# The forget gate's summed rows: eight transfers within SBUF in place of matmuls and copies

## The chip, the cores and the metric

One core of one Trainium2 chip. The metric is the device time of one execution in microseconds (us), the median of the runs shown.

## The reference, cut to what matters

A stack of layers in float32 for 512 tokens: an even layer (forget-gate attention and latent attention), an odd layer, two convolutional feed-forward parts, a delta-rule layer and an MLP. The change lies in the even layer's attention with a forget gate. Eight heads of width 64; each head has one gate value for each token, and the running sum of its logarithm enters every score:

```python
log_f = jax.nn.log_sigmoid((fg + b_forget).astype(jnp.float32))
...
c = jnp.cumsum(log_f, axis=1).transpose(0, 2, 1)
...
logits = jnp.einsum('bqhd,bkhd->bhqk', qb, k).astype(jnp.float32) * scale
logits = logits + cq[..., :, None] - c[..., None, :]
logits = jnp.where(mask, logits, NEG_INF)
p = jax.nn.softmax(logits, axis=-1).astype(v.dtype)
```

The term cq is the same for a whole row of the softmax and drops out; the kernel adds only the negated sum by key, `-c[k]`. A tile of scores has queries on the partitions and keys along the free dimension, so each of its 128 partitions needs the same row of 512 values, a different one for each head.

## The kernel before, in words

Activations lie with features on the partitions, x and hH/hL as [128, 8, 512]. Products in float32 are made of three matmuls on rounded high and low parts (`three`, lines 474 to 476). Weights come in units of up to 1024 KB: SP loads a unit into one of two raw buffers (line 406) as soon as the split of the unit that used it is done (semaphore w_split), ACT rounds it to wH (two halves, `even_hi`), DVE subtracts to wL (`lo_half`, line 2022), PE multiplies.

The order of the even layer is written out by hand as slots. PE walks t from 32 to 239; each t is one step of a projection (for even_in one of eight k steps of a tile, 16 slots a unit), and pair_events(t) puts the attention's work ahead of that step. ACT and DVE walk the same t from 34 on with their parts of the same slots. A tile of attention is a pair of heads g = m // 4 and a block of 128 queries, largest first: m = 0 to 15 are the forget-gate heads, pair_slot(m) = 48, 55, 62, 69 for the first pair, 76, 83, 90, 97 for the second, 104, 111, 118, 125 for the third, 147 and on for the fourth. At slot s PE makes both heads' scores (`pair_scores`, L749, mask L754), after waiting that DVE is done with head 1 of the tile before (line 729, event pair.biased); DVE adds the bias and takes the row's minimum (`pair_biased`, L2306), waiting for gate.bias of both heads; ACT takes the exponential at s + 1; DVE divides at s + 4 (L2315, L2317, events pair.prob); at s + 7 PE transposes (`pair_turn`, L767), ACT copies, and after four tiles PE multiplies by the values (L778).

The bias. DVE's gate chain (lines 2347 to 2359) runs on eight partitions, one for each head: minimum, log-sigmoid with ACT's help, a running sum along the tokens (L2356), a negation (L2357). The negated sums are rounded by ACT and the remainder made by DVE (L2359), into gate_split, two float32r rows for each head. At gate_slot(h) = 43, 45, 66, 68, 88, 90, 106, 108, PE spreads head h to all partitions (`gate_spread`, L788 and L789): the row is picked by a column of the identity, in two matmuls over 8 partitions, into bank 7; ACT copies the bank to cB (`gate_bias`), which has room for two pairs of heads. From the third pair on ACT first waits until pair.biased of the last tile of the pair two before is there, since its row of cB is written again. `a`, ACT's helper, is line 1330 for all of its activations. `rank_sums`, at slot 116, uses bank 7 next and waits for the last gate.bias.

Other transfers that stay inside SBUF: at slot 146 ACT issues two (line 1650) that copy the rotated key rows, 32 partitions, into kM, four times each; SP issues eight of 32 partitions into qM (line 450). ACT's queue also carries rope (line 1579), dist and the constants of the later layers.

Of the kernel before, what the change touches and what calls it, by code (L numbers as in the profile page):

```python
# [21 lines left out]
F32 = mybir.dt.float32  # L22
F32R = mybir.dt.float32r
# [4 lines left out]
P = 128  # L28
# [69 lines left out]
class Events:  # L98
# [22 lines left out]
    def at(self, event, i=None):  # L121
        if self.known is None:
            return self.sem("first_build"), 1
        name, value, stride = self.known[event]
        if i is None:
            return self.sem(name), value
        return self.sem(name), i * stride + value
# [26 lines left out]
def build(nc, dram, known):  # L154
    ctx = ExitStack()
    with ctx:
# [7 lines left out]
        def sb(name, shape, dt=F32, where=None):  # L164
            size = 4 * int(np.prod(shape[1:]))
            if where is None:
                where = place[0]
                place[0] += size
            assert where + size <= nc.sbuf_usable_end, (name, where + size - nc.sbuf_usable_end)
            return nc.alloc_sbuf_tensor_at(name, shape, dt, offset=where)  # L170
# [34 lines left out]
        cq_at, qF_at = base + 4 * 5 * SEQ, base + 4 * (13 * SEQ + 2 * 1280)  # L205
        cqRaw = sb("cqRaw", [P, 5, SEQ], F32, cq_at)
        foxH, foxL = sb("foxH", [P, 4, SEQ], F32R, qF_at), sb("foxL", [P, 4, SEQ], F32R, qF_at + 4 * 4 * SEQ)
        gate_split = sb("gate_split", [P, 2, SEQ], F32R, qF_at + 4 * 16 * SEQ)
        qM, kM = sb("qM", [P, H, SEQ], F32, h_at), sb("kM", [P, H, SEQ], F32, h_at + 4 * H * SEQ)
        mH, mL, ft = stage([("mH", [P, MLP_GROUP, SEQ], F32R), ("mL", [P, MLP_GROUP, SEQ], F32R), ("ft", [P, 8, SEQ])])  # L210
        vO, dist, probO, lamt, dH, dL, qk = stage([
# [70 lines left out]
        def gate_slot(h):  # L282
            return (43, 66, 88, 106)[h // 2] + 2 * (h % 2)
# [184 lines left out]
        def _(pe):  # L468
# [310 lines left out]
                                  start=j == 0, stop=j == TT - 1, skip_group_check=True)  # L779
                last.then_inc(*tick("pair_pe", f"pair.values{g}"))  # L780

            def gate_spread(h):

                pe.wait_ge(*at("gate.rows"))
                if h:
                    pe.wait_ge(*at(f"gate.bias{h - 1}"))
                pick = identR[0:H, h:h + 1].to_broadcast([H, P])
                mm(bank[7][:], pick, gate_split[0:H, 0, :], start=True, stop=False)  # L788
                mm(bank[7][:], pick, gate_split[0:H, 1, :], start=False, stop=True).then_inc(*tick("gate_pe", f"gate.spread{h}"))  # L789

            def rank_sums():

                pe.wait_ge(*at(f"gate.bias{H - 1}"))
                for c, what in enumerate(("cq", "ckv")):
                    pe.wait_ge(*at(f"{what}.squares"))
                    for t in range(TT):
                        last = mm(bank[7][:, 4 * c + t:4 * c + t + 1], (sq[:, 0, :], ss)[c][:, t * P:(t + 1) * P], ones[:, 0:1],
                                  start=True, stop=True)
                last.then_inc(*tick("sums_pe", "cq.sums"))

            def pair_events(t):

                for m in pairs_at(t, 0):
                    pair_scores(m)
                for g in pair_ends(t, 9):
                    pair_values(g)
                for m in pairs_at(t, 7):
                    pair_turn(m)
                for h in range(H):
                    if gate_slot(h) == t:  # L810
                        gate_spread(h)

            def first_ready(k):

# [513 lines left out]
        def _(act):  # L1328
# [249 lines left out]

            act.dma_start(rope[:], dram["rope"]).then_inc(*tick("loaded_rope", "in.rope", 16))

            act.wait_ge(*at("gate.min"))
            gate_log = prob[0:H, 0, 0:512]
            a(gate_log, misc[0:H, :], ACT.Abs, bias=v("b_forget")[0:H, :]).then_inc(*tick("gate_act", "gate.abs"))
# [1 line left out]
            a(gate_log, gate_log, ACT.Exp, scale=-1.0).then_inc(*tick("gate_act", "gate.exp"))  # L1585
            act.wait_ge(*at("gate.exp"))
            a(gate_log, gate_log, ACT.Ln, bias=1.0).then_inc(*tick("gate_act", "gate.ln"))
            act.wait_ge(*at("gate.negative"))
            a(gate_split[0:H, 0, :], prob[0:H, 1, 512:1024], ACT.Copy).then_inc(*tick("gate_act", "gate.hi"))

            def even_hi(n, f):

# [21 lines left out]
            def pair_hi(g):  # L1614

                act.wait_ge(*at(f"pair.values{g}"))
                a(foxH[:, g, :] if g < 4 else hH[:, 2 * g - 8, :], bank[6][:], ACT.Copy).then_inc(*tick("pair_act", f"pair.hi{g}"))

            def gate_bias(h):

                act.wait_ge(*at(f"gate.spread{h}"))
                if h >= 4:
                    act.wait_ge(*at(f"pair.biased{4 * (h // 2 - 2) + 3}.1"))
                a(cB[:, h // 2 % 2, h % 2, :], bank[7][:], ACT.Copy).then_inc(*tick("gate_act", f"gate.bias{h}"))

            def rank_square(k):

# [6 lines left out]
            for t in range(34, 240):  # L1634
# [32 lines left out]
                        pair_copy(m)  # L1667
                for m in pairs_at(t, 1):
                    pair_exp(m)
                for h in range(H):  # L1670
                    if gate_slot(h) == t:
                        gate_bias(h)
                for m in pairs_at(t, 7):
# [328 lines left out]
        def _(dve):  # L2002
# [342 lines left out]
                tt(sq[:, g, :], sq[:, g, :], ss[:], ALU.add).then_inc(*tick("rope_dve", f"rope.rotated{g}"))  # L2345

            even_evict(0)
            gate_log, gate_z, gate_one, gate_neg = (prob[0:H, e, 512 * c:512 * c + 512] for e in range(2) for c in range(2))
            dve.wait_ge(evac, 1)
            nc.vector.memset(gate_one, 1.0)  # L2350
            chain(ts(gate_z, misc[0:H, :], v("b_forget")[0:H, :], 0.0, ALU.add, ALU.min), "gate_dve", "gate.min")
# [2 lines left out]
            dve.wait_ge(*at("gate.ln"))  # L2354
            chain(tt(gate_z, gate_z, gate_log, ALU.subtract), "gate_dve", "gate.logf")
            chain(nc.vector.tensor_tensor_scan(gate_log, gate_one, gate_z, 0.0, ALU.mult, ALU.add), "gate_dve", "gate.summed")  # L2356
            ts(gate_neg, gate_log, -1.0, None, ALU.mult).then_inc(*tick("gate_dve", "gate.negative"))  # L2357
            dve.wait_ge(*at("gate.hi"))
            tt(gate_split[0:H, 1, :], gate_neg, gate_split[0:H, 0, :].bitcast(F32), ALU.subtract).then_inc(*tick("gate_dve", "gate.rows"))  # L2359
            for t in range(34, 240):  # L2360
                if t % 8 == 0 and 40 <= t <= 144:
                    even_evict(t // 8 - 1)
# [651 lines left out]
```

## Time and profile before

| | us |
|---|---|
| median of 3 runs | 2013.41 |
| lowest, highest | 2012.32, 2014.16 |
| span of the profiled execution | 2010.4 |
| PE busy | 1991.0 |
| DVE busy | 1149.2 |
| ACT busy | 820.8 |
| POOL busy | 3.8 |

The profiled execution is given by its span, from its first to its last instruction; the median of the runs is 3.0 us more, which is what lies around a span. The mean granted clock of PE is 0.998. PE's matmul durations overlap: two matmuls of 0.39 us start 0.23 us apart, so positions are read by starts. Line 1330 stands for every ACT activation; tiles tell them apart.

### The profile page before, as it was taken

Reading aid. Unit: us, or ns where it says so; the run is one execution under the profiler, and the core shown is the slowest. Engines: PE = TensorE matmul, PEld = TensorE weight load, DVE = VectorE, ACT = ScalarE, POOL = GpSimd, SP = SyncE. Lnnn points to the kernel's source line nnn. Section 1 sums busy time; section 2 is a strip of 40 time slices with the busy share of each in tenths; the row PEclk is TensorE's granted clock in tenths of the full one; section 3 lists DMA queues with packets and bytes.
Section 4 is the critical chain, followed back from the end, with each engine's and each line's share of the span. In section 5 each row is a group of like instructions: output and inputs, shape, how many; then the busy total and the mean of one; then the engine's idle time right before and its main releaser. Section 6 shows DMA issues by size and latency. Waiting matters only on the chain.

```text
span 2010.4 us, 30047 instructions
## 1 busy us (share of the span) xinstructions
PE 1991.0 (99%) x11917; PEld 1608.7 (80%) x11917; DVE 1149.2 (57%) x1896; ACT 820.8 (41%) x1293; POOL 3.8 (0%) x6
## 2 busy tenths in 40 slices
PE   9999999999999999999999999999999999999998
PEld 6776798888888787888888888777777578888888
DVE  6456467534556666567543555877666566424532
ACT  6447544333334454454332333643443432212322
POOL 0000000000000000000000000000000000000000
PEclk9999999999999999999999999999999999999999
DMA  5112122223323211122223224111111122322221
GB/s 192 64 53 84 43 85 92 86 95 105 104 79 110 69 64 64 63 85 86 97 95 102 102 77 142 42 62 33 57 43 44 45 84 103 105 87 102 88 100 63
DMA packets 26992, 165.58 MB, mean 82 GB/s; under 512 B 3200, under 2 KB 3328, under 8 KB 11008
## 3 DMA queue, kind: packets, MB, share of 16 engines
q1 hardware_dynamic: 25872, 161.69, 23.4%
q10 hardware_dynamic: 1008, 2.30, 0.4%
q8 instruction: 82, 1.34, 0.3%
q14 instruction: 30, 0.25, 0.0%
HBM read 160.83 MB, written 2.10 MB: 81 GB/s over the span
## 4 chain that ended last, share of the span: by engine, by line
PE 89%; DVE 6%; ACT 3%; issue 1%; DMA 0%; SPq 0%; DVEq 0%; ACTq 0%
PE bank L474 25%; PE bank L476 24%; PE bank L475 24%; PE bank L1133 2%; PE bank L749 1%; ACT hH L1330 1%; DVE hL L2102 1%; PE bank L957 1%; PE bank L778 1%; PE bank L981 1%; ACT wH L1330 1%; DVE x L2098 1%; PE bank L767 1%; PE bank L1222 1%; PE bank L1220 1%
## 5 line engine op out<-in xcount | busy, mean ns | idle before, releaser
L474 PE MATMUL bank<-hH,wH 128*128 128x512 f32 x1368 | 552.0, 404 | 1.5 <-DVE hL L2064 1.5
L476 PE MATMUL bank<-hH,wL 128*128 128x512 f32 x1368 | 533.7, 390 | 0.0
L475 PE MATMUL bank<-hL,wH 128*128 128x512 f32 x1368 | 533.1, 390 | 0.0
L1330 ACT ACTIVATE wH<-raw 128x2048 fp32r<-128x2048 f32 (+3 forms) x199 | 294.1, 1488 | 116.3 <-PE bank L476 105.1
L474 PEld LDWEIGHTS bank<-hH,wH 128*128 128x128 f32 x1368 | 257.6, 188 | 69.0 <-issue 14.5
L476 PEld LDWEIGHTS bank<-hH,wL 128*128 128x128 f32 x1368 | 257.4, 188 | 54.4
L475 PEld LDWEIGHTS bank<-hL,wH 128*128 128x128 f32 x1368 | 257.9, 189 | 46.1
L2013 DVE TENSOR_TENSOR wL<-raw,wH 128x2048 fp32r<-128x2048 f32 x96 | 219.7, 2289 | 125.6 <-ACT wH L1330 125.6
L474 PE MATMUL bank<-mH,wH 128*128 128x512 f32 (+1 forms) x610 | 233.1, 382 | 0.0
L476 PE MATMUL bank<-mH,wL 128*128 128x512 f32 (+1 forms) x610 | 232.9, 382 | 0.0
L475 PE MATMUL bank<-mL,wH 128*128 128x512 f32 (+1 forms) x610 | 232.9, 382 | 0.0
L474 PEld LDWEIGHTS bank<-mH,wH 128*128 128x128 f32 x610 | 114.7, 188 | 22.2
L475 PEld LDWEIGHTS bank<-mL,wH 128*128 128x128 f32 x610 | 114.7, 188 | 22.0
L476 PEld LDWEIGHTS bank<-mH,wL 128*128 128x128 f32 x610 | 114.7, 188 | 22.0
L1330 ACT ACTIVATE y<-bank 128x512 f32<-128x512 f32 (+4 forms) x132 | 57.8, 464 | 150.3 <-PE bank L476 89.0
L2022 DVE TENSOR_TENSOR wL<-raw,wH 128x1024 fp32r<-128x1024 f32 x76 | 92.0, 1218 | 22.3 <-ACT wH L1330 22.1
L2418 DVE TENSOR_TENSOR ft<-bank,dg 128x512 f32<-128x512 f32 x44 | 30.4, 690 | 86.2 <-PE bank L476 86.2
L1330 ACT ACTIVATE ft<-ft 128x512 f32<-128x512 f32 x44 | 27.8, 632 | 116.6 <-DVE ft L2423 116.6
L1330 ACT ACTIVATE ft<-ft,vec 128x512 f32<-128x512 f32 x44 | 35.8, 815 | 86.5 <-DVE ft L2418 86.5
L1330 ACT ACTIVATE mH<-y 128x512 f32 (+1 forms) x32 | 20.2, 632 | 120.9 <-DVE y L2841 120.9
L1330 ACT ACT_TABLE_LOAD x47 | 60.3, 1283 | 1.7 <-PEq L3005 0.7
L474 PE MATMUL bank<-wH,hH 128*128 128x256 f32 x192 | 57.5, 299 | 0.0
(346 smaller groups left out, 2790.5 us busy)
## 6 DMA issues: line engine op xcount, KB each, us to landing
raw<-in_ffn_up SPq DMA_DIRECT2D x44, 1024.0 KB, 4.8
raw<-in_mlp_up SPq DMA_DIRECT2D x16, 1024.0 KB, 4.9
raw<-in_mlp_down SPq DMA_DIRECT2D x16, 1024.0 KB, 4.9
raw<-in_ffn_down SPq DMA_DIRECT2D x16, 768.0 KB, 4.2
raw<-in_odd_in SPq DMA_DIRECT2D x12, 1024.0 KB, 4.8
raw<-in_dn_qkv SPq DMA_DIRECT2D x12, 1024.0 KB, 4.9
raw<-in_ffn_down SPq DMA_DIRECT2D x16, 640.0 KB, 3.8
raw<-in_even_in SPq DMA_DIRECT2D x7, 1024.0 KB, 4.8
```

The source lines that it names most:

```text
L474: mm(out, a, c, start=first, stop=False, skip_group_check=joined)
L475: mm(out, a, d, start=False, stop=False, skip_group_check=joined)
L476: return mm(out, b, c, start=False, stop=last, skip_group_check=joined)
L749: last = mm(bank[2 + e][:, 0:n], q, k, start=True, stop=g >= 4)
L767: last = nc.tensor.transpose(bank[4 + e][:, j * P:(j + 1) * P], pair_tile(e, i)[:, j * P:(j + 1) * P], ident)
L778: last = mm(bank[6][half(e), j * P:], (vF if g < 4 else vM)[:, j, head(g % 4, e)], PT[:, e, j, j * P:], start=j == 0, stop=j == TT - 1, sk ...
L957: last = mm(bank[2 + e][:, 0:n], qk[half(e), h % 2, 0, i * P:n], qk[half(e), h % 2, 1, 0:n], start=True, stop=True)
L1133: last = mm(bank[b][part(e), chunk(n)], left[part(e), chunk(n)], right[part(e), chunk(n)], start=True, stop=True)
L1330: return nc.scalar.activation(out, in_, func, **kw)
L2013: tt(wL[s][:], raw[s][:], wH[s][:].bitcast(F32), ALU.subtract).then_inc(w_split, 1)
L2022: ins = tt(wL[n % 2][:, cols], raw[n % 2][:, cols], wH[n % 2][:, cols].bitcast(F32), ALU.subtract)
L2418: tt(gate, bank[b0][:], rinv, ALU.mult).then_inc(evac, 1)
```

## The change

gate_split becomes gate_rows, a plain float32 tile, into whose first eight partitions DVE writes the negated sums. ACT's rounding and DVE's subtraction go. PE's gate_spread goes, and with it the wait of rank_sums. gate_bias(h) on ACT is no longer a copy from PSUM: it issues a transfer from partition h of gate_rows, repeated 128 times, to the same place in cB (256 KB). The first four are issued in one go right behind the gate chain, ahead of ACT's first slot; heads 4 to 7 keep their slots 88, 90, 106 and 108 and their wait. Each transfer has its own semaphore, which counts 16. DVE's waits in pair_biased are the same events.

```diff
-        gate_split = sb("gate_split", [P, 2, SEQ], F32R, qF_at + 4 * 16 * SEQ)
+        gate_rows = sb("gate_rows", [P, SEQ], F32, qF_at + 4 * 16 * SEQ)
...
-            def gate_spread(h):
-
-                pe.wait_ge(*at("gate.rows"))
-                if h:
-                    pe.wait_ge(*at(f"gate.bias{h - 1}"))
-                pick = identR[0:H, h:h + 1].to_broadcast([H, P])
-                mm(bank[7][:], pick, gate_split[0:H, 0, :], start=True, stop=False)
-                mm(bank[7][:], pick, gate_split[0:H, 1, :], start=False, stop=True).then_inc(*tick("gate_pe", f"gate.spread{h}"))
-
             def rank_sums():
 
-                pe.wait_ge(*at(f"gate.bias{H - 1}"))
...
-                for h in range(H):
-                    if gate_slot(h) == t:
-                        gate_spread(h)
...
+            def gate_bias(h):
+
+                if h >= 4:
+                    act.wait_ge(*at(f"pair.biased{4 * (h // 2 - 2) + 3}.1"))
+                act.dma_start(cB[:, h // 2 % 2, h % 2, :], gate_rows[h:h + 1, :].unsqueeze(1).to_broadcast([1, P, SEQ]))\
+                    .then_inc(*tick(f"gate_loaded{h}", f"gate.bias{h}", 16))
+
...
-            act.wait_ge(*at("gate.negative"))
-            a(gate_split[0:H, 0, :], prob[0:H, 1, 512:1024], ACT.Copy).then_inc(*tick("gate_act", "gate.hi"))
+            act.wait_ge(*at("gate.rows"))
+            for h in range(4):
+                gate_bias(h)
...
-            def gate_bias(h):
-
-                act.wait_ge(*at(f"gate.spread{h}"))
-                if h >= 4:
-                    act.wait_ge(*at(f"pair.biased{4 * (h // 2 - 2) + 3}.1"))
-                a(cB[:, h // 2 % 2, h % 2, :], bank[7][:], ACT.Copy).then_inc(*tick("gate_act", f"gate.bias{h}"))
...
-                for h in range(H):
+                for h in range(4, H):
                     if gate_slot(h) == t:
                         gate_bias(h)
...
-            ts(gate_neg, gate_log, -1.0, None, ALU.mult).then_inc(*tick("gate_dve", "gate.negative"))
-            dve.wait_ge(*at("gate.hi"))
-            tt(gate_split[0:H, 1, :], gate_neg, gate_split[0:H, 0, :].bitcast(F32), ALU.subtract).then_inc(*tick("gate_dve", "gate.rows"))
+            ts(gate_rows[0:H, :], gate_log, -1.0, None, ALU.mult).then_inc(*tick("gate_dve", "gate.rows"))
```

## Rows read from the trace of the kernel before

**Rows 1.** The page: span, busy time of the engines.

```profile
span 2010.4 us, 30047 instructions
PE 1991.0 (99%) x11917; PEld 1608.7 (80%) x11917; DVE 1149.2 (57%) x1896; ACT 820.8 (41%) x1293; POOL 3.8 (0%) x6
```

**Rows 2.** Window in the even layer: length, busy time and count of PE, PEld, DVE, ACT, POOL, then PEclk, DMA share, GB/s.

```profile
46.00:56.00 10.00, 10.00 (x79) 8.72 (x76) 6.58 (x15) 5.59 (x12) 0.00 (x0) 1.00 0.12 48
```

**Rows 3.** Instructions of line 788: durations in ns, first and last start in us.

```profile
L788 PE MATMUL bank<-gate_split,constR x8: 475/493/497, 40.4 to 111.3; 8*128 8x512 f32 x8
```

**Rows 4.** Timeline of PE around the second spread: start, us, engine, line, what.

```profile
42.07 0.39 PE L475 MATMUL bank<-hL,wH 128*128 128x512 f32 x1
42.30 0.40 PE L476 MATMUL bank<-hH,wL 128*128 128x512 f32 x1
...
43.62 0.39 PE L475 MATMUL bank<-hL,wH 128*128 128x512 f32 x1
```

**Rows 5.** Timeline of ACT: the gate's rounding and the wH of unit 3.

```profile
38.98 0.63 ACT L1330 ACTIVATE gate_split<-prob 8x512 fp32r<-8x512 f32 x1 [2.44 <-DVE prob L2357]
39.52 1.99 ACT L1330 ACTIVATE wH<-raw 128x1024 fp32r<-128x1024 f32 x2
```

**Rows 6.** Timeline of ACT: the two issues of line 1650, and what stood behind them.

```profile
150.20 1.38 ACTq L1650 DMA_DIRECT2D kM<-misc  x2
151.63 0.59 ACT L1330 ACTIVATE kM<-bank 64x512 f32<-64x512 f32 x1 [1.72 <-issue]
```

**Rows 7.** Timeline of DVE, from the split of unit 3 to head 3 of the second group.

```profile
40.59 2.36 DVE L2022 TENSOR_TENSOR wL<-raw,wH 128x1024 fp32r<-128x1024 f32 x2 [0.27 <-ACT wH L1330]
...
47.59 0.69 DVE L2306 CUSTOM_DVE_ANT_0 prob<-bank,cB 128x512 f32<-128x512 f32 x1
...
49.47 0.89 DVE L2317 TENSOR_SCALAR prob<-prob,stat 128x512 f32<-128x512 f32 x2
...
58.43 0.75 DVE L2317 TENSOR_SCALAR prob<-prob,stat 128x384 f32<-128x384 f32 x2
...
75.68 0.69 DVE L2306 CUSTOM_DVE_ANT_0 prob<-bank,cB 128x512 f32<-128x512 f32 x1
```

**Rows 8.** Timeline of PE: first step of unit 3, transposes of tiles 0 and 1.

```profile
46.88 0.33 PE L474 MATMUL bank<-wH,hH 128*128 128x256 f32 x1
...
53.18 1.06 PE L767 MATMUL bank<-const,prob 128*128 128x128 f32 x8
...
60.10 0.84 PE L767 MATMUL bank<-const,prob 128*128 128x128 f32 x6
```

**Rows 9.** DMA issues of the whole run: tile, queue, count, KB each, median us from issue to landing.

```profile
qM<-sq SPq DMA_DIRECT2D x8, 64.0 KB, 2.0
kM<-misc ACTq DMA_DIRECT2D x2, 256.0 KB, 3.7
dist<-in_dist ACTq DMA_DIRECT2D x1, 256.0 KB, 2.5
raw<-in_even_in SPq DMA_DIRECT2D x7, 1024.0 KB, 4.8
```

**Rows 10.** Windows: both kM transfers in flight, a 1024 KB weight load.

```profile
152.00:152.50 0.50, 0.50 (x4) 0.46 (x5) 0.20 (x1) 0.49 (x2) 0.50 (x2) 1.00 0.94 180
177.00:178.00 1.00, 1.00 (x6) 0.73 (x4) 0.42 (x2) 0.99 (x4) 0.00 (x0) 1.00 0.98 418
```

**Rows 11.** Window at the end of the run, behind the last matmul.

```profile
2008.00:2009.00 1.00, 0.00 (x0) 0.00 (x0) 0.00 (x0) 0.00 (x0) 0.00 (x0) 0.50 1.01 410
```

**Rows 12.** Timelines of ACT, DVE and PE at the third group.

```profile
88.89 0.60 ACT L1330 ACTIVATE cB<-bank 128x512 f32<-128x512 f32 x1 [2.28 <-PE bank L789]
...
106.42 0.68 DVE L2306 CUSTOM_DVE_ANT_0 prob<-bank,cB 128x512 f32<-128x512 f32 x1
...
108.28 0.88 DVE L2317 TENSOR_SCALAR prob<-prob,stat 128x512 f32<-128x512 f32 x2
...
115.37 1.06 PE L767 MATMUL bank<-const,prob 128*128 128x128 f32 x8
```

More of the change, by code:

```diff
@@ L2347, in _ @@
             even_evict(0)
-            gate_log, gate_z, gate_one, gate_neg = (prob[0:H, e, 512 * c:512 * c + 512] for e in range(2) for c in range(2))
+            gate_log, gate_z, gate_one = (prob[0:H, c // 2, 512 * (c % 2):512 * (c % 2) + 512] for c in range(3))
             dve.wait_ge(evac, 1)
```

## The prediction

> **What bounds the kernel now.** The page comes first: PE is busy 1991.0 of 2010.4 us, no other engine over 57% [rows 1]. A window inside the even layer says the same of the stage that is changed: PE busy all of 10 us, at clock 1.00, with 48 GB/s on the DMA engines [rows 2]. So PE's instruction stream is the clock of this stage, and what PE doesn't execute is time gained, as long as nothing that PE waits for comes later. Then come the timelines of each engine from 38 to 62 us, and the table of DMA issues. The profiled execution is known by its span, 2010.4 us; the median of the three runs is 3.0 us above it, and I carry that 3.0 along.
>
> **What is removed.** The first spread runs at 40.4, the last at 111.3 us, eight in all [rows 3]. In PE's timeline two matmuls of the projection start 0.23 us apart; around a spread, from L476 at 42.30 to the L475 two places on, 1.32 us pass where 0.46 would [rows 4]. So a spread costs 0.86 us, with the switches to and from eight-row weights. Two spreads lie ahead of the first group's softmax: 1.7 us. Six lie behind it; three of them stand beside transposes, scores or values, where PE pays a switch anyway (I take off 0.1 each): 4.8 us. In all 6.5 us of PE time. ACT loses one rounding (0.63 us [rows 5]) and eight copies of 0.60 us, DVE one subtraction; both have idle time, so I count nothing for these. rank_sums loses a wait that was long satisfied: nothing.
>
> **What is added on ACT's queue.** The first four transfers are issued in a row as soon as the negated sums are there, where the rounding began, at 38.98 us [rows 5]. Two issues took 1.38 us and the next activation waited behind them [rows 6]. Four take 2.8, so ACT is at 41.8 where it was at 39.52 [rows 5]. Queued behind them on ACT: both halves of wH of unit 3 (2.0 us), on which DVE's split waits (2.36 us from 40.59 [rows 7]); it would end about 45.2 instead of 42.95. PE wants unit 3 at 45.2 (46.88 [rows 8] less two spreads), so the price is 0 to 0.2 us and disappears in what comes next. SP's next weight load is released by the same split and comes 2.3 us later; it takes 4.8 us [rows 9] and its data are used 20 us on: nothing. The table puts no transfer of SP beside the first two, and POOL has nothing here.
>
> **How long a transfer takes.** This is the price that decides. All of the 256 KB of one transfer are read from one partition (row h, 128 times 2 KB). The trace has no such transfer, so it is bounded. Fixed part: 64 KB within SBUF land 2.0 us after the issue [rows 9]; I take 2.0. Moving part, lower bound: the rate of a load into 128 partitions, 418 GB/s [rows 10], 0.6 us; dist, with the same 256 KB in the same rows of 2 KB, lands in 2.5 [rows 9]. The nearest rows are the two kM transfers: inside SBUF, the same queue, 2 KB pieces, each source row read four times, but 32 partitions on either side. There the DMA engines are busy 0.94 of the time and yet move 180 GB/s, less than half of 418 [rows 10], and they land in 3.7 [rows 9]. So with fewer partitions the sixteen engines stand in each other's way. Upper bound: in proportion to partitions, 180/32 = 5.6 GB/s, 47 us. Between: 128 to 32 partitions cost a factor 2.3; the same factor for each further fourfold step (two and a half of them) gives 180/8.0 = 22 GB/s, and a sixteenth of 418, one engine's share, is 26. I take **26 GB/s, 10 us for a transfer**, since both ways of going on from the nearest rows come out near it (11.7 by the other).
>
> The Trainium skill, page "SBUF — State Buffer", section "Door 1: The DMA port swizzle", says that a transfer's rate depends on how many of 16 ports its partitions reach, 8 for 32 partitions and one for four or fewer, and gives 27.6 GB/s measured for partitions 0 to 3. By it a transfer would move for an estimated 9.5 us and the sum would be 1 us less. The halving in the kM rows agrees with it; that reading alone, with writes spread over all partitions, obeys it too is shown by no row.
>
> **Where it lands on the path.** The transfers share one queue and neighbouring source partitions, so they follow each other and land at 39.0 + 2.0 + 10, 20, 30, 40, that is at 51, 61, 71 and 81 us. DVE needs the second for head 1 of the first tile (L2306 at 47.59 [rows 7]). It waits until 61. Behind it on DVE stand the division of tile 0, the split of unit 4, an eviction and the second tile; ACT waits for DVE with the exponential, and behind that the wH of unit 4. PE waits first in the scores of tile 1 (line 729) at about 50.5, then in the transposes of tile 0. In the trace the products end 2.77 us after the start of that L2306 (47.59 to 50.36 [rows 7]), so 63.8 now; the transposes of head 0 may start 0.4 earlier, at 63.4, against 53.18 before [rows 8]: **+10.2 us**. DVE then still has the splits of unit 4, an eviction and the rotary of the keys between it and the products of tile 1; those ended at 59.18 [rows 7], 0.9 before PE used them at 60.10 [rows 8], and I estimate them 1.3 us later against PE: +0.4.
> PE stands still for some 11 us. At the end of the run, in a window without a matmul, its clock is granted at 0.50 (1.2 of 2.4 GHz) [rows 11], where it was 1.00 in the layer [rows 2], so it will come back from the stall at the lower level. No row shows how soon it rises again. Bounds: 0, and all of the 6.9 us from tile 0's transposes to tile 1's [rows 8] at half speed, 6.9. I take 2, nearer the low end, because part of that stretch is semaphore and switch time, which a clock doesn't stretch.
> Second group (heads 2, 3, landed at 81): first wanted both at 75.68 [rows 7], now later by 10.6 + 2 - 1.7: 87. Hidden. Third group: ACT can issue head 4 at about 86.6, where it now begins to wait (88.89 - 2.28 [rows 12]), head 5 behind the square of the second tile; both have landed 22 us later, at 108.6 on the old scale. The spreads of heads 4 and 5 are gone from in between, so on that scale DVE wants them at 104.7, not 106.42, and waits 3.9. The products end 2.74 us after the bias (109.16 less 106.42 [rows 12]), now at 111.3, and PE, four spreads earlier than 115.37 [rows 12], wants them at 112.0: 0.7 in hand. SP loads weights in the same stretch, so I count +0.5. Fourth group: over 35 us of lead, nothing.
>
> Sum: + 10.2 + 0.4 + 2 + 0.5 - 4.8 (the six later spreads; the first two are inside the 10.2) = **+8.3 us**: span 2018.7, time 2021.7.
>
> **The rivals.**
> - **Hidden (faster).** Only writing suffers from few partitions, and the kM rows, which have 32 on both sides, can't tell. Then a transfer moves in 0.6 to 1.4 us, the first two land by 44, DVE needs them at 46 at the soonest, and the 6.5 us of spreads come out less 0.2: 2007.1. It decides in this way as long as head 1 lands before 49 (PE's transposes of tile 0 at 53.18 less 1.7, less the 2.4 from landing to transposes), that is below 4 us a transfer; the change breaks even at some 6.5. For it: kM's 3.7 us to landing, and that nothing else loads in that stretch. Against it: engines 0.94 busy at less than half the rate. The Trainium skill, page "DMA: Bandwidth & Descriptors", section "Anatomy of one DMA", gives (for the gpsimd path) 2.0 us plus bytes over 436 GB/s, an estimated 2.6 us for 256 KB; dist in the trace agrees, kM does not.
> - **One partition is much slower than a sixteenth.** At 20 us a transfer head 1 lands at 81 (+30.6), heads 2 and 3 at 121 where 107 is wanted (+14), the third group waits 24 less 4.6 of slack (+19), the fourth +1; with clock and spreads +62: 2075. Against it: it needs a limit that the kM rows do not show.
> - **Not what it says.** If the broadcast were read once and written 128 times, it is the hidden case.
>
> **How the numbers follow.** A sixteenth of the rate or near it: 0.58; hidden: 0.28; much slower: 0.10; break-even, some 6.5 us a transfer: 0.04. About 0.2% (4 us) is what a measurement can tell. Faster 0.30 (the hidden case and half of the break-even), within 0.2% 0.04 (the rest, and the low edge of the likeliest), slower 0.66. The likeliest case reaches from 2017 (9 us a transfer, no clock) to 2036 (about 13 us: +6 at head 1, +5 at the third group, 2 more for the clock). The range has to take in the hidden case as well: 2006 to 2036, with the much slower case left out.
>
> **What would show it.** Landing times of the first four transfers in steps of 10 us, with the DMA share near 1 at about 26 GB/s; L2306 waiting for the transfers from 46 to 61; PE idle about 11 us before line 749 of tile 1, the granted clock below 1 behind it; no stall at the second group. PE's stream 6.5 us shorter and no gap would make the prediction wrong, and so would landing times of 3 us. If PE waited for wL of unit 3, the four issues would be the price.

## The result, and the profile after

| | before | after |
|---|---|---|
| median | 2013.66 (4 runs) | 2025.04 (4 runs) |
| lowest, highest | 2012.32, 2014.16 | 2023.58, 2026.65 |
| span of the profiled execution | 2010.4 | 2024.8 |

The changed kernel is slower: ratio 1.0057, with a 95% interval of 1.0044 to 1.0070, or +11.4 us by the medians. The two profiled executions differ by 14.4 us in span. The one of after is the longest of its four runs (2026.65 us) and 1.85 us above its span; in the other runs of both kernels, too, the time is only some 1.8 to 2.2 us above the span. So not all of the 3.0 us that the prediction carried lies around a span: about one is that the execution of before was a short one, and some 3 us of the 14.4 are scatter. The forecast was +8.3.

The page of after, where [rows 1] stood before:

```profile
span 2024.8 us, 30001 instructions
...
PE 1987.4 (98%) x11901; PEld 1609.3 (79%) x11901; DVE 1148.4 (57%) x1895; ACT 816.0 (40%) x1284; POOL 3.8 (0%) x6
...
PE bank L474 25%; PE bank L476 23%; PE bank L475 23%; PE bank L1120 2%; PE bank L749 1%; ACT hH L1317 1%; DVE hL L2090 1%; PE bank L944 1%; ACT wH L1317 1%; PE bank L778 1%; PE bank L968 1%; ACTq L1572 1%; DVE x L2086 1%; PE bank L767 1%; PE bank L1209 1%
```

PE is busy 3.6 us less and the span is 14.4 us longer. In the chain by line, a DMA issue of ACT has come in, ACTq L1572, which is the transfer of gate_bias. So time is lost in issuing. The transfers by tile (line, queue, count, durations of the issues in ns, first and last start in us; below, from issue to landing):

```profile
L1572 ACTq DMA_DIRECT2D cB<-gate_rows x8: 477/600/9608, 38.7 to 123.1; - x8
...
DMA to landing us min/median/max: 11.8/18.6/32.6
```

One issue took 9.6 us where 0.7 was reckoned (half of the 1.38 of [rows 6]). The chain that ended last, in order of time, from the gate chain to the first scores (start, us, what):

```profile
38.65 0.59 ACTq L1572
39.28 0.61 ACTq L1572
39.92 6.77 ACTq L1572
46.71 9.61 ACTq L1572
56.42 1.06 ACT wH L1317
57.51 0.98 DVE wL L2010
58.50 0.16 issue
58.65 1.23 DVE wL L2010
59.93 2.08 PE bank L749 x4
```

Two issues pass in 0.6 us each, the third holds ACT for 6.8, the fourth for 9.6: 17.7 us in all. Behind them on ACT stands the wH of unit 3, behind it on DVE the split to wL, and behind that PE. Its timeline (start, us, engine, line, tiles; in brackets the idle time before and what ended it):

```profile
43.05 0.39 PE L476 MATMUL bank<-hH,wL 128*128 128x512 f32 x1
59.93 2.08 PE L749 MATMUL bank<-kF,qF 64*128 64x512 f32 x4 [16.49 <-DVE wL L2010]
...
70.38 1.06 PE L767 MATMUL bank<-const,prob 128*128 128x128 f32 x8
```

PE stands still for 16.5 us. The transposes of tile 0 come at 70.38, at 53.18 before [rows 8]. Windows of the stretch (columns as in rows 2):

```profile
46.00:50.00 4.00, 0.00 (x0) 0.00 (x0) 0.00 (x0) 0.00 (x0) 0.00 (x0) 0.50 0.88 27
50.00:52.00 2.00, 0.00 (x0) 0.00 (x0) 0.00 (x0) 0.00 (x0) 0.00 (x0) 0.50 0.95 29
...
64.00:66.00 2.00, 2.00 (x12) 2.00 (x11) 1.24 (x4) 2.00 (x4) 0.00 (x0) 0.50 0.92 28
66.00:68.00 2.00, 2.00 (x18) 2.00 (x18) 0.95 (x1) 0.59 (x1) 0.00 (x0) 0.96 0.88 27
```

From 46 to 56 us all five engines are idle, and the DMA engines are some 0.9 busy for 25 to 29 GB/s. That is about the rate that was forecast. The granted clock is 0.50 in the stall and stays there for the first six microseconds of work.

The path can be followed by the starts of the transposes (L767), after less before. They stood at 53.18 and 115.37 before [rows 8, 12]; now at 70.38 and 127.56, so +17.2 and +12.2. The scores ahead of the first came 14.4 later (45.55 before, 59.93 now). So: 14.4 us by the stall, with two spreads already taken off; 2.8 more in the stretch at half clock; 5.0 given back by the six later spreads; and then, by the next transposes (124.07 before, 138.45 now), +14.4 again. These last 2.2 us are lost while heads 6 and 7, the fourth pair, are issued. ACT's timeline there, then PE's:

```profile
122.56 0.72 ACT L1317 ACTIVATE prob<-prob,stat 128x512 f32<-128x512 f32 x1 [1.50 <-DVE stat L2294]
122.56 6.93 ACTq L1572 DMA_DIRECT2D cB<-gate_rows  x2
...
129.60 1.09 ACT L1317 ACTIVATE y<-bank 128x512 f32<-128x512 f32 x2 [5.22 <-PE bank L767]
```

```profile
132.04 0.95 PE L787 MATMUL bank<-const,sq 128*128 128x1 f32 x8
133.51 1.05 PE L787 MATMUL bank<-const,ss 128*128 128x1 f32 x8 [0.52 <-DVE ss L2367]
```

The issue of head 7 takes 6.4 of the 6.93 us, the exponential of the next tile comes late, DVE's sum of squares behind it too, and PE waits 0.5 us; the granted clock is 0.61 and 0.54 in the four microseconds from 134 us. That this makes up the 2.2 us is read from this one trace: in the first experiment below head 7's issue is held 6.3 us in the same way, the clock stays at 1.00 from 126 to 136 us, and only 0.6 us are lost.

### The profile page after: what moved, and what is told of

The parts are those of the page before. It is cut to its first block, busy times and chain, and to the rows that moved or that the text cites. A ratio compares the mean times of both kernels' runs of the same rounds, so it can differ in the third digit from the quotient of the medians.

```text
span 2024.8 us, 30001 instructions
## 1 busy us (share of the span) xinstructions
PE 1987.4 (98%) x11901; PEld 1609.3 (79%) x11901; DVE 1148.4 (57%) x1895; ACT 816.0 (40%) x1284; POOL 3.8 (0%) x6
## 4 chain that ended last, share of the span: by engine, by line
PE 86%; DVE 6%; ACT 4%; issue 2%; ACTq 1%; DMA 1%; SPq 0%; DVEq 0%
PE bank L474 25%; PE bank L476 23%; PE bank L475 23%; PE bank L1120 2%; PE bank L749 1%; ACT hH L1317 1%; DVE hL L2090 1%; PE bank L944 1%; ACT wH L1317 1%; PE bank L778 1%; PE bank L968 1%; ACTq L1572 1%; DVE x L2086 1%; PE bank L767 1%; PE bank L1209 1%
```

## The experiments

Theory A, from the chain: a queue takes only so many slow transfers; the issues hold ACT, and that is the price. Theory B, the prediction's: the landing of head 1 holds DVE. A third question is what makes a transfer slow. Each edit is against the changed kernel unless another is named. Each ratio is to runs of the kernel before made beside that experiment, whose medians lie between 2013.03 and 2014.18 us.

Spans scatter for a reason far from the change. In a later layer, some 1305 us into the run, PE waits once for DVE's rowsG. Of the following lines the first is of the last experiment, the second of the first kernel with eight sources (who waits for whom, total, times, longest):

```profile
PE bank L1141 <- DVE rowsG L2619: 1.8, 1, 1.8
PE bank L1141 <- DVE rowsG L2618: 3.1, 1, 3.1
```

Where it is 3.1, the granted clock goes down to about 0.50 behind it, and from there to the end the run takes some 1.5 or 3.0 us more than the 701.6 of the others. It is 1.8 in the traces of before, after, the first and the last experiment and 3.1 in the nine others; what decides it wasn't looked into. So the table behind the last experiment compares the even layer alone.

### Two issued behind the gate chain, two later

```diff
-            for h in range(4):
+            for h in range(2):
                 gate_bias(h)
...
+                if t == 44:
+                    gate_bias(2)
+                    gate_bias(3)
```

> Only the place of the issues of heads 2 and 3 is changed: ACT issues heads 0 and 1 behind the gate chain, heads 2 and 3 at its slot 44, behind the rounding of unit 3. Theory A (a transfer from one partition moves at 26 to 29 GB/s, and ACT can't begin a third one before the first is nearly drained, so the four issues in a row held up the weights of unit 3): two issues of 0.6 us, unit 3 rounded by 42, no wait of PE for wL at slot 48; now the landing of head 1 at about 60 holds DVE, PE stands still before the scores of tile 1, its transposes of tile 0 start near 63.4 instead of 70.4 in the changed kernel, and the run is 4 to 7 us faster than the changed kernel, about 2018 to 2021. Theory B (the landing of head 1 at 60 binds anyway and the held issues cost nothing of their own): the same time as the changed kernel, within 1.5 us of 2025.

Measured: 2021.9 us, ratio 1.0041 [1.0027, 1.0056], span 2018.1. Timelines of DVE, PE and ACT:

```profile
51.13 0.69 DVE L2297 CUSTOM_DVE_ANT_0 prob<-bank,cB 128x512 f32<-128x512 f32 x1 [6.08 <-DMA cB<-gate_rows]
...
61.27 0.69 DVE L2297 CUSTOM_DVE_ANT_0 prob<-bank,cB 128x512 f32<-128x512 f32 x1 [9.44 <-DMA cB<-gate_rows]
```

```profile
62.02 1.65 PE L749 MATMUL bank<-kF,qF 64*128 64x384 f32 x4 [11.54 <-DVE stat L2297]
...
64.09 1.93 PE L767 MATMUL bank<-const,prob 128*128 128x128 f32 x8
```

```profile
40.52 6.58 ACTq L1572 DMA_DIRECT2D cB<-gate_rows  x1
...
47.13 8.92 ACTq L1572 DMA_DIRECT2D cB<-gate_rows  x1
```

The wait for wL is gone and the one that the prediction describes stands in its place: DVE waits until 61.3 (forecast 61), PE stands still 11.5 us in the scores of tile 1 (forecast some 11) and makes the transposes of tile 0 at 64.1 (forecast 63.4). The transposes of tile 1 are at 72.05 against 60.10 [rows 8], +12.0 where the prediction's terms give 12.6. The two later issues are held 6.6 and 8.9 us as before; they only no longer stand ahead of unit 3. Both mechanisms are real; the held issues hide the late landing, because the earlier stall lets head 1 arrive in time. Taking the first off the path saves 6.7 us of span, not 16. By the medians it is 2.5 us (+8.9 against +11.4, each to its own runs of before) where 4 to 7 were expected, and the two intervals overlap: that one stall takes the other's place is shown by the traces, its worth by them alone.

### A source on 128 partitions

```diff
-                act.dma_start(cB[:, h // 2 % 2, h % 2, :], gate_rows[h:h + 1, :].unsqueeze(1).to_broadcast([1, P, SEQ]))\
+                act.dma_start(cB[:, h // 2 % 2, h % 2, :], x[:, h, :])\
```

> The eight transfers keep their size, queue, order and destination, but read x (128 partitions, 2 KB of each) in place of one partition of the gate's rows, so the bias added to the scores is not the gate's. Theory A (the single source partition sets the rate, and the slow drain is what holds the issues): each lands in 2.5 to 3.7 us, each issue takes 0.5 to 0.7 us, PE has no wait in the even layer that it didn't have before, and the time is the before kernel's less the spreads, 2006 to 2008. Theory C (the rate is set by the writes, by the queue of ACT or by transfers inside SBUF as such): landings stay near 10 us apart and the time near 2025.

This kernel leaves out the gate's bias and adds x in its place; it is for timing alone, as are the next two. Measured: 2008.25 us, ratio 0.9974 [0.9963, 0.9985]. The transfers by tile, a window in which they are in flight, and PE's wait:

```profile
L1572 ACTq DMA_DIRECT2D cB<-x x8: 472/521/634, 38.6 to 104.9; - x8
...
DMA to landing us min/median/max: 2.3/2.5/5.1
```

```profile
40.00:41.00 1.00, 1.00 (x6) 0.80 (x6) 0.00 (x0) 0.00 (x0) 0.00 (x0) 1.00 1.01 379
```

```profile
PE bank L749 <- DVE wL L2010: 1.4, 1, 1.4
```

The same bytes to the same places at 379 GB/s, landed in 2.5 us, and no issue above 0.63. Now the change is a gain. The long issues come from the slow transfers, not from their number alone: four in a row took 2.5 us (forecast 2.8). But PE still waits 1.4 us for wL, where the prediction had 0 to 0.2.

### Four source partitions, side by side or four apart

```diff
+                act.dma_start(cB[:, h // 2 % 2, h % 2, :], x[0:4, h:h + 1, :].to_broadcast([4, P // 4, SEQ]))\
```

```diff
+                act.dma_start(cB[:, h // 2 % 2, h % 2, :], x[0:16:4, h:h + 1, :].to_broadcast([4, P // 4, SEQ]))\
```

> As e2, but the source is x on partitions 0 to 3, each row read 32 times; the bias is again not the gate's. Theory A1 (neighbouring partitions share one way out, as the page on the port swizzle has it): still 26 to 29 GB/s, landings 9 to 10 us apart, time near 2025. Theory A2 (each single partition has a limit of its own, about 28 GB/s): four times the rate, 256 KB in 2.3 us, landings near 4.5 us after the issue, time near 2007.

> As e3, but on partitions 0, 4, 8 and 12. Both A1 and A2 expect about 105 to 115 GB/s: 256 KB move in 2.3 to 2.5 us, landings 4.5 us after the issue, and a time near 2007 to 2009. If it is as slow as e3, the number of source partitions or of DMA engines used counts, and not which partitions they are.

Measured, one run each: 2021.22 us for partitions 0 to 3, 2011.28 for 0, 4, 8 and 12. A window with the transfers in flight, of the first and then of the second, and the four issues of the first:

```profile
42.00:44.00 2.00, 1.66 (x8) 1.04 (x6) 0.00 (x0) 0.00 (x0) 0.00 (x0) 1.00 0.23 25
```

```profile
40.00:41.00 1.00, 1.00 (x6) 0.84 (x5) 0.00 (x0) 0.00 (x0) 0.00 (x0) 1.00 0.26 102
```

```profile
38.86 9.92 ACTq L1572 DMA_DIRECT2D cB<-x  x4
```

Both keep about a quarter of the DMA engines busy (share 0.23 and 0.26), and the one moves 25, the other 102 GB/s. A single source partition, with a share of 0.8 to 1.0, moved 25 to 29 in most windows. So the limit is neither the engines nor the single partition, but a way out that four neighbouring partitions share: 25 to 29 GB/s, and four such ways 102. The Trainium skill, page "SBUF — State Buffer", section "Door 1: The DMA port swizzle", puts partitions 0 to 3 on one of 16 ports, with 27.6 GB/s, and 0, 4, 8 and 12 on four; these two windows agree with it, and for reads.

The issues don't follow the rate alone. The longest is 9.6 us for one partition, 4.1 for four side by side and 1.3 for four apart; but one partition and four side by side drain equally fast (25 to 29 and 25 GB/s), and yet the four issues take 17.7 us in the one case and 9.9 in the other. That is why the first of these kernels came out near 2021 and not at the 2025 that was expected: PE waits 8.7 us for wL in place of 16.5, and then the landing of head 1 is what binds, with tile 0's transposes at 64.08, as in the first experiment (64.09). The second is above its expectation of 2007 to 2009: four issues take 4.3 us and PE waits 3.1 for wL.

### Eight sources for each head

The gate's weight columns are laid out so that head h's gate comes out on eight partitions, four apart; the gate chain runs on 64 partitions in place of 8, at the same durations.

```diff
-                act.dma_start(cB[:, h // 2 % 2, h % 2, :], gate_rows[h:h + 1, :].unsqueeze(1).to_broadcast([1, P, SEQ]))\
+                o = 32 * (h // 4) + h % 4
+                act.dma_start(cB[:, h // 2 % 2, h % 2, :], gate_rows[o:o + 32:4, :].unsqueeze(1).to_broadcast([8, 16, SEQ]))\
...
-    misc = np.concatenate([w[:, cuts[2]:cuts[2] + 64], kr, kr[:, 16:], kr[:, :16]], 1)
+    copies = [4 * (p // 32) + p % 4 for p in range(64)]
+    misc = np.concatenate([w[:, cuts[2]:cuts[3]][:, copies], kr, kr[:, 16:], kr[:, :16]], 1)
```

> The changed kernel with one thing else: the weight columns of the gate are laid out so that each head's gate is computed on eight partitions four apart (64 partitions in all, the same instructions), and each transfer reads these eight, 16 times each. The result is the reference's. Theory A1 (partitions four apart have ways out of their own, 26 GB/s each): about 200 GB/s, 256 KB in 1.3 us, landings 3.3 to 3.7 us after the issue, four issues of 0.6 us in a row, PE waits 1.5 us for wL of unit 3 as in e2 and for nothing else new: 2007 to 2009, 0.2 to 0.3% faster than before. If something about a gate row that the chain has just written counts, and not its partitions: near 2020.

> e5 with heads 2 and 3 issued at ACT's slot 44, behind the rounding of unit 3, as in e1. By the account of e2 this takes 1.2 us off ACT's queue ahead of unit 3 and so most of PE's 1.5 us wait: 2006 to 2008, 1 us faster than e5. If the wait has another cause, the same as e5.

The second of the two also has heads 2 and 3 at slot 44, as in the first experiment. Measured: 2010.69 us, ratio 0.9982 [0.9973, 0.9992]; and 2007.57, 0.9968 [0.9956, 0.9981]. A window of the first, and its wait; then the wait of the second:

```profile
40.00:41.00 1.00, 1.00 (x6) 0.84 (x5) 0.00 (x0) 0.00 (x0) 0.00 (x0) 1.00 0.53 166
```

```profile
PE bank L749 <- DVE wL L2011: 2.3, 1, 2.3
```

```profile
PE bank L749 <- DVE wL L2014: 0.7, 1, 0.7
```

About half of the engines are busy and move 135 to 166 GB/s, less than twice the rate of four and below the 200 that was expected. The four issues take 3.4 us where four of 0.6 were expected. No wait for a landing is left; what remains is the wait for unit 3, which shrinks from 2.3 to 0.7 us when two issues move behind its first half. The longer wait costs more than its length. Behind it, in the first kernel:

```profile
46.00:48.00 2.00, 2.00 (x8) 1.25 (x7) 1.16 (x4) 0.00 (x1) 0.00 (x0) 0.50 0.93 271
```

In the second the clock is 1.00 in that window, and tile 0's transposes come at 51.47 where they are at 54.44 in the first, 3.0 us for 1.6 us less of waiting.

### By way of HBM

```diff
-                act.dma_start(cB[:, h // 2 % 2, h % 2, :], gate_rows[h:h + 1, :].unsqueeze(1).to_broadcast([1, P, SEQ]))\
+                act.dma_start(cB[:, h // 2 % 2, h % 2, :], gate_hbm[h:h + 1, :].unsqueeze(1).to_broadcast([1, P, SEQ]))\
...
+            act.dma_start(gate_hbm[:], gate_rows[0:H, :]).then_inc(*tick("gate_stored", "gate.stored", 16))
+            act.wait_ge(*at("gate.stored"))
```

> The changed kernel with the rows stored to HBM first (16 KB, one more transfer and a wait of ACT for it) and the eight transfers reading one row of HBM 128 times. If only a single SBUF partition is slow to read: the store lands at 41, each transfer moves at 200 to 400 GB/s and lands in 2.5 to 3.5 us, ACT is held for 2 us by the store and 2.4 by the issues, unit 3's wL is 3.5 to 4 us late at PE: about 2010. If repeated reads of one 2 KB place are slow wherever they are: landings 10 us apart, and above 2025.

Measured: 2010.81 us, ratio 0.9977 [0.9966, 0.9989]. Window:

```profile
43.00:44.00 1.00, 0.64 (x3) 0.19 (x1) 0.00 (x0) 1.00 (x2) 0.00 (x0) 1.00 1.00 354
```

One HBM row read 128 times moves at 354 GB/s, so a source read many times is not slow by itself; it is slow where it is one partition of SBUF. The store in front (issued at 38.85, first broadcast at 40.35) costs ACT 1.5 us, and PE waits 2.8 us for wL; the granted clock is 0.50 from 46 to 52 us behind it.

### Two heads by PE, six by slow transfers

The kernel before, with its spreads for heads 0 and 1 (both on gate_split as before), and heads 2 to 7 by the change's transfer from one partition, each at a slot of its own:

```diff
-                for h in range(H):
-                    if gate_slot(h) == t:
+                for h in range(H):
+                    if (43, 45, 46, 60, 78, 86, 100, 112)[h] == t:
                         gate_bias(h)
```

> The kernel before, in which only heads 2 to 7 come by the slow transfers from one partition, issued one at a time at ACT's slots 46, 60, 78, 86, 100 and 112, at least 8 us apart and 12 us or more before their use; heads 0 and 1 stay two spreads on PE. Theory A (the slow rate costs only where a landing or a held issue is on the path): six spreads less and nothing waits: 4 to 5 us faster than before, about 2008 to 2009, though each transfer still lands in 11 to 12 us. If slow transfers cost by themselves (by slowing the weight loads that share the engines): no gain, or slower.

Measured: 2008.36 us, ratio 0.9971 [0.9962, 0.9981]. The transfers by tile:

```profile
L1627 ACTq DMA_DIRECT2D cB<-gate_rows x6: 477/480/589, 43.1 to 111.3; - x6
...
DMA to landing us min/median/max: 11.1/11.3/12.2
```

One at a time, the same transfer is issued in 0.5 us and lands in 11.3, and nothing waits for it. Six spreads less give 5.1 us by the medians. A load of 1024 KB beside them landed after 12.7 us in place of 4.8, and that was hidden too. So it is not the slow transfer that costs, but its being wanted 8 us after the row is there, and its being issued where earlier ones have not drained.

### The four issues on SP's queue

```diff
+                        if n == 5:
+                            sp.wait_ge(*at("gate.rows"))
+                            for h in range(4):
+                                sp.dma_start(cB[:, h // 2 % 2, h % 2, :], gate_rows[h:h + 1, :].unsqueeze(1).to_broadcast([1, P, SEQ]))\
+                                    .then_inc(*tick(f"gate_loaded{h}", f"gate.bias{h}", 16))
...
-            for h in range(4):
-                gate_bias(h)
```

> The changed kernel with the first four transfers issued by SP, ahead of its load of unit 5, in place of ACT; source, size and order are the same. If it is the issuing queue that is held while earlier transfers of it drain: SP's third and fourth issue take 6.5 and 9 us in its turn, ACT rounds unit 3 at 39 at once, PE has no wait for wL at slot 48, and DVE waits for head 1 until 60 as in e1; transposes of tile 0 near 63.5; the load of unit 5 is issued 11 us late (56 in place of 45) and lands in time for ACT's slot 66. Time 2019 to 2022, about that of e1. If it is something of ACT: SP's issues take 0.6 us each.

Measured: 2027.15 us, ratio 1.0067 [1.0052, 1.0083]. The chain, SP's part of it, and PE's second stop:

```profile
40.35 6.75 SPq L443
47.14 9.59 SPq L443
56.77 26.38 DMA raw<-in_even_in
```

```profile
87.75 0.68 PE L772 MATMUL bank<-const,prob 128*128 128x128 f32 x2 [2.40 <-DVE prob L2308]
```

The holds are the same to 0.02 us on another engine's queue, so they come from the transfers and not from ACT. ACT is free now and the first stall is that of the first experiment (11.1 us). But SP's own next load, of unit 5, goes out at 56.8 in place of some 43, and lands 26.4 us later, behind the broadcasts of its own queue; a load takes 4.8 otherwise [rows 9]. ACT waits 8.65 us for it before it can round the unit, PE stops once more for 2.4 us, and its clock falls a second time (0.50 from 88 to 90 us). By the transposes of the next pair's first tile this kernel is 4.3 us behind the first experiment (98.08 and 93.83), from 0.6 ahead at tile 0. The expectation of 2019 to 2022 had no such second stop.

### PE kept at work through the stall

The first experiment, with 46 matmuls into an idle bank ahead of the scores of tile 1.

```diff
+                if t == 55:
+                    for n in range(46):
+                        mm(bank[7][:], hH[:, 0, 0:P], hH[:, 0, :], start=True, stop=True)
```

> e1 with 46 matmuls more on PE, written to bank 7 and used by nobody, ahead of the scores of tile 1, where PE stands still from 50.5 to 62 in e1. They take 46 x 0.227 = 10.4 us of a stall of 11.5. If the clock at 0.50 behind the stall costs time: the granted clock stays at 1.00 up to 61, the work from 62 to 66 runs at full speed, and the run is 2 us (1 to 3) faster than e1's 2021.9. If it costs nothing: within 0.7 us of e1, or slower by what the extra matmuls overrun.

Measured: 2021.08 us, ratio 1.0039 [1.0024, 1.0055], beside 1.0041 without them. Windows:

```profile
62.00:64.00 2.00, 1.61 (x8) 0.92 (x9) 1.08 (x6) 1.91 (x4) 0.00 (x0) 0.96 0.81 25
64.00:66.00 2.00, 2.00 (x12) 2.00 (x11) 2.00 (x5) 1.74 (x3) 0.00 (x0) 0.50 1.02 31
66.00:68.00 2.00, 2.00 (x14) 2.00 (x14) 1.97 (x5) 1.38 (x5) 0.00 (x0) 0.69 0.88 27
```

The clock stays up through the stall and falls all the same at 64, after two short stops at 61 and 63 us. From the scores of tile 1 to the transposes of tile 1 it is 10.1 us with the matmuls and 10.0 without (62.11 to 72.21, 62.02 to 72.05), and 8.05 in the kernel before (52.05 to 60.10). The dip moved; the run was 0.8 us faster where 1 to 3 was expected if the clock costs time and up to 0.7 if it doesn't, and it decides nothing, since the clock fell in both.

### Eight sources, all issued behind unit 3's first half

```diff
+                if t in (36, 44):
+                    for h in range(2):
+                        gate_bias(h + (t == 44) * 2)
```

With the sources of the eight-fold layout, and the issues ahead of ACT's first slot taken out.

> e6 with heads 0 and 1 issued behind ACT's rounding of unit 3 as well (ACT's slot 36; heads 2 and 3 at slot 44). PE's wait for wL of unit 3 (0.7 us in e6) goes; heads 0 and 1 are issued at about 41 and land at 44.5 to 45.5, ahead of DVE's use at 46. By this account 2006 to 2008, up to 1 us faster than e6. If the landings come after 47, DVE waits for them, PE's slack of 3 us at the transposes hides up to 3 us of it, and the time is that of e6.

Measured: 2005.75 us against 2014.18, ratio 0.9966 [0.9952, 0.9979]. ACT, DVE, PE:

```profile
39.39 1.06 ACT L1317 ACTIVATE wH<-raw 128x1024 fp32r<-128x1024 f32 x1 [2.45 <-DVE gate_rows L2347]
39.48 1.24 ACTq L1573 DMA_DIRECT2D cB<-gate_rows  x1
```

```profile
45.51 0.69 DVE L2296 CUSTOM_DVE_ANT_0 prob<-bank,cB 128x512 f32<-128x512 f32 x1 [0.62 <-PE bank L754]
```

```profile
51.71 1.06 PE L767 MATMUL bank<-const,prob 128*128 128x128 f32 x8
```

ACT starts the wH of unit 3 where it did before [rows 5], DVE waits for PE again and not for a transfer, and the transposes of tile 0 come 1.5 us earlier than in [rows 8]. By the transposes at the layer's end (131.44 before, 124.97 here) it is 6.5 us ahead, and 6.5 in span: the whole of the eight spreads. This version beats both kernels. Its ratio can't be told from that of the second eight-source kernel (0.9968); that PE's 0.7 us of wait are gone is read from the trace.

All kernels side by side, in us against before: by the medians, each to its own runs of before; and by one trace each over the stretch that the change touches, from the last projection matmul ahead of tile 0's scores (at 45.23 before) to the last transposes of the fourth pair of heads (137.70 before). The 1.7 us of the two spreads ahead of the stretch are counted as gained where they are gone.

| | by the medians | by the stretch |
|---|---|---|
| after | +11.4 | +14.8 |
| two issued, two later | +8.9 | +7.6 |
| wide source | -4.8 | -5.3 |
| partitions 0 to 3 | +8.2, one run | +7.7 |
| partitions 0, 4, 8, 12 | -1.8, one run | -2.0 |
| eight sources | -2.8 | -2.9 |
| eight sources, two later | -5.9 | -5.9 |
| by way of HBM | -2.7 | -1.0 |
| two by PE | -5.1 | -5.0 |
| SP's queue | +13.0 | +11.2 |
| PE kept at work | +6.9 | +7.1 |
| eight sources, all behind | -8.4 | -6.7 |

## Why the prediction was right or wrong

**The spreads, 6.5 us, 1.7 ahead and 4.8 behind:** right. Six gave 5.1 by the medians and 5.0 by the stretch of the table, all eight 6.5 by position, and in the changed kernel 5.0 came back between tile 0 and the third pair of heads.

**The rate of one source partition, 26 GB/s:** right, 25 to 29, though it was taken between two ways of going on from rows of 32 partitions and no row had this case. The first landed 11.9 us after its issue, the others in steps of 9.6: 50.6, 60.2, 69.8 and 79.3, forecast 51, 61, 71 and 81. The rival in which only writing suffers from few partitions would have landed by 44 and is ruled out by the windows; twice as slow is ruled out by the same ones.

**The issues, "Four take 2.8, so ACT is at 41.8": the step that failed.** They took 17.7. The 2.8 was twice the two kM issues of [rows 6], which drain at 180 GB/s [rows 10]; for transfers that drain at 27 it doesn't hold. Four that drain at 379 GB/s did take 2.5. The rate is not all of it: four from partitions 0 to 3, at 25 GB/s, took 9.9. Behind it the split of unit 3 was not 2.3 us late but 17, and "0 to 0.2 us" became a stall of 16.5. The prediction had named the sign of it, "If PE waited for wL of unit 3, the four issues would be the price", without a price for it.

**The moment at which PE wants unit 3, 45.2:** wrong as well, in little. It was read from the first step of unit 3, but PE already stops ahead of the scores of the same slot, at 43.4. That is why even 2.5 us of issues cost 1.4 us in the wide-source run, and why moving them behind wH is worth something.

**The wait of DVE for head 1, +10.2 and +0.4:** not what happened in the changed kernel, where head 1 was there 2.9 us before its bias at 63.06. Right in the kernel in which the held issues are off the path: tile 0 at +10.9, tile 1 at +12.0, clock included, and a span 7.7 us above before (8.9 by the medians) where +8.3 was the sum.

**The clock, +2, bounds 0 to 6.9:** 2.8 us between scores and transposes of tile 0 (10.45 us where it was 7.63), and 2.0 in the first experiment between scores and transposes of tile 1 (10.03 where it was 8.05). Nearer the low end, as taken; that it is the clock alone is read from windows and not separated by a run.

**The third group (pair of heads), DVE waits 3.9, +0.5:** DVE waited 1.6 us and PE not at all.

**The fourth group, nothing:** wrong for the same reason as the first. The landing is hidden, the issue isn't: 6.4 us of ACT for head 7, and 2.2 us at the transposes behind it, most of them with the clock near 0.5; 0.6 in the first experiment, where the clock stayed up.

So the sum against the span: 14.4 (stall less two spreads) + 2.8 − 5.0 + 2.2 = +14.4, where 10.2 + 0.4 + 2 + 0.5 − 4.8 = +8.3 stood. That the total was near is in part luck: the term that was put at nothing took the place of another of nearly its size. Both grow as the transfers drain more slowly, but not in a fixed proportion, as the four neighbouring partitions show. Two small things in the working: the top of the range, by its own terms (6, 5 and 2 on 2021.7), is 2035 and not 2036, and the 3.0 us around a span are some 2.

## What to carry to other kernels

A row that goes to all partitions by a transfer within SBUF goes out by one narrow way; spread its copies over partitions four apart where they are made, or send it by HBM. Count the issue of a transfer as cheap only where the ones ahead of it on its queue have drained or drain fast: otherwise the issuing engine can be held for microseconds (up to 9.6 here), and so is all that stands behind it on that engine. Put urgent work ahead of the issues, and keep to one slow transfer at a time: the kernel that did so, each transfer issued 8.5 us or more after the one before, had no held issue.

## What the runs showed of the hardware

- An issue is no constant. Of four equal transfers in a row from one partition the third held the queue 6.8 and the fourth 9.6 us, on ACT as on SP. The releases (46.7 and 56.3) come 3.9 us ahead of the landings of the first and second. How much a queue takes is not settled: in the first group two passed, in the fourth the second was held 6.4 us although head 5 had landed at 121.7, before head 6 was issued; and at the same rate of draining four issues took 17.7 us from one partition and 9.9 from four neighbours.
- Reads within SBUF: 25 to 29 GB/s from one partition or four neighbours, 102 from four partitions four apart, 135 to 166 from eight, 379 from 128. Eight fall short of twice four, and why wasn't tried.
- The busy share of the DMA engines follows the outermost size of the source pattern: 0.23 to 0.26 for four partitions, 0.53 for eight, and 0.8 to 1.0 for one partition repeated 128 times. For the one partition the full share gained nothing over the quarter that partitions 0 to 3 had (25 to 29 and 25 GB/s).
- Slow transfers hold up loads on either queue: with them on ACT's queue, SP's 1024 KB load took 19.8 us to land in the changed kernel (issued at 59.90) and 17.5 in the first experiment (at 43.87), and 26.4 behind them on SP's own, where it takes 4.8 otherwise [rows 9].
- A short stop of PE can cost more than itself: 2.3 us of waiting and the clock at 0.50 behind it put tile 0's transposes 3.0 us behind those of the kernel with 0.7 us of waiting and the clock at 1.00.
